# Attention on one core: the transposes of a tile's weights issued in front of the scores of the tile three ahead

## The reference, cut to what matters

```python
def one_chunk(args):
    j, q_j = args                       # 64 queries, the 8 chunks before them and their own
    k_j = lax.dynamic_slice_in_dim(k_pad, j * CHUNK, BAND, axis=1)
    v_j = lax.dynamic_slice_in_dim(v_pad, j * CHUNK, BAND, axis=1)
    s = jnp.einsum('bqhd,bkhd->bhqk', q_j, k_j) * scale + bias
    s = jnp.where(valid, s, jnp.float32(-1e30))
    p = jax.nn.softmax(s, axis=-1)
    return jnp.einsum('bhqk,bkhd->bqhd', p, v_j)
...
o = o * jax.nn.silu(g)                  # gate; then a product with w_out
```

## Time and profile before

| what | value |
|---|---|
| median of 3 runs | 2435.27 us (2433.29 to 2435.69) |
| profiled execution, first to last instruction (span) | 2432.2 us |
| PE, PEld busy | 2397.0 us (99%), 2050.3 us (84%) |
| DVE, ACT, POOL busy | 1591.1 us (65%), 1173.4 us (48%), 1212.6 us (50%) |
| chain that ended last, share on PE | 85% |
| mean granted TensorE clock | 0.997 |

### The profile page before, as it was taken

One profiled execution on the slowest core, in us unless ns is written; L12 is line 12 of the kernel. 1 busy time (PEld: TensorE's weight loads), 2 busy tenths in 40 slices (PEclk: granted clock), 3 DMA queues, 4 the chain that ended last, 5 costly groups with the idle time before them and its releaser, 6 DMA issues.

```text
span 2432.2 us, 36012 instructions
## 1 busy us (share of the span) xinstructions
PE 2397.0 (99%) x13552; PEld 2050.3 (84%) x13552; DVE 1591.1 (65%) x2151; ACT 1173.4 (48%) x2308; POOL 1212.6 (50%) x883
## 2 busy tenths in 40 slices
PE   7999999999999999999999999999999999999999
PEld 6888898875578898899888889999988888888887
DVE  6966757488544286653667775777434489888863
ACT  5322223334444253322445556788534434888861
POOL 1644445431044445544455545666444546866664
PEclk9999999999999999999999999999999999999999
DMA  7454544494133344543333448665234253300034
GB/s 278 156 192 150 188 152 160 152 314 143 36 108 127 129 153 153 190 158 113 104 104 104 104 117 234 160 155 144 76 115 165 99 173 111 104 1 1 5 127 156
DMA packets 295724, 329.21 MB, mean 135 GB/s; under 512 B 88264, under 2 KB 226304, under 8 KB 293760
## 3 DMA queue, kind: packets, MB, share of 16 engines
q1 hardware_dynamic: 294080, 326.81, 41.9%
q10 hardware_dynamic: 1472, 0.10, 0.0%
HBM read 247.53 MB, written 79.33 MB: 134 GB/s over the span
## 4 chain that ended last, share of the span: by engine, by line
PE 85%; DVE 7%; ACT 3%; issue 2%; DMA 1%; POOL 1%; SPq 0%; DVEq 0%; ACTq 0%
PE ps L1239 22%; PE ps L1241 22%; PE ps L1240 22%; PE ps L1576 3%; PE ps L1747 2%; PE ps L1728 2%; PE ps L1491 2%; PE ps L1510 2%; PE ps L1562 2%; PE ps L1504 1%; DVE s_raw L2433 1%; PE ps L1259 1%; PE ps L1474 1%; PE ps L1447 1%; DVE s_lo L2420 1%
## 5 line engine op out<-in xcount | busy, mean ns | idle before, releaser
L1125 POOL TENSOR_TENSOR w_lo<-raw,w_hi 128x512 fp32r<-128x512 f32 (+1 forms) x450 | 643.4, 1438 | 798.9 <-ACT w_hi L1853 762.9
L1853 ACT ACTIVATE w_hi<-raw 128x512 fp32r<-128x512 f32 (+1 forms) x454 | 281.3, 628 | 776.2 <-PE ps L1241 628.8
L1239 PE MATMUL ps<-w_hi,s_hi 128*128 128x256 f32 (+2 forms) x832 | 262.8, 316 | 0.6 <-DVE u L2553 0.3
L1240 PE MATMUL ps<-w_lo,s_hi 128*128 128x256 f32 (+2 forms) x832 | 262.0, 315 | 0.0
L1241 PE MATMUL ps<-w_hi,s_lo 128*128 128x256 f32 (+2 forms) x832 | 262.0, 315 | 0.0
L1125 POOL TENSOR_TENSOR w_lo<-raw_wide,w_hi 128x512 fp32r<-128x512 f32 x112 | 157.1, 1412 | 149.6 <-ACT w_hi L1853 149.6
L2553 DVE TENSOR_TENSOR u<-u,ps 128x1024 f32<-128x1024 f32 (+1 forms) x96 | 116.4, 1212 | 142.4 <-PE ps L1241 138.8
L1239 PE MATMUL ps<-w_hi,a_hi 128*128 128x256 f32 (+2 forms) x624 | 197.0, 316 | 0.6 <-POOL w_lo L1125 0.6
L1240 PE MATMUL ps<-w_lo,a_hi 128*128 128x256 f32 (+2 forms) x624 | 196.6, 315 | 0.0
L1241 PE MATMUL ps<-w_hi,a_lo 128*128 128x256 f32 (+2 forms) x624 | 196.6, 315 | 0.0
L1239 PE MATMUL ps<-s_hi,w_hi 128*128 128x512 f32 x480 | 188.6, 393 | 3.2 <-DVE s_lo L2420 2.3
(11 more groups left out here) (349 smaller groups left out, 6244.2 us busy)
## 6 DMA issues: line engine op xcount, KB each, us to landing
raw<-in_w SPq DMA_DIRECT2D x158, 512.0 KB, 4.2
ada_c<-in_ada SPq DMA_DIRECT2D x14, 2304.0 KB, 10.5
blk<-u SPq DMA_DIRECT2D x46, 512.0 KB, 4.3
raw_wide<-in_w SPq DMA_DIRECT2D x32, 512.0 KB, 4.6
blk<-c SPq DMA_DIRECT2D x23, 512.0 KB, 3.3
blk<-m1s SPq DMA_DIRECT2D x23, 512.0 KB, 3.3
ada_first<-in_ada SPq DMA_DIRECT2D x12, 768.0 KB, 16.2
r_g<-blk SPq DMA_DIRECT2D x8, 1024.0 KB, 9.3
```

The costliest lines, as they stand in the source:

```text
L1125: pool.tensor_tensor(w_ring(w_lo, n), w_source(n), w_ring(w_hi, n).bitcast(F32), ALU.subtract)\
L1239: pe.matmul(out, a_hi_, b_hi_, start=first, stop=False, skip_group_check=True)
L1240: pe.matmul(out, a_hi_, b_lo_, start=False, stop=False, skip_group_check=True)
L1853: act.activation(w_ring(w_hi, n), w_source(n), ACT.Copy).then_inc(w_rounded, 1)
```

## The change

In every step e of the loop the call of `a_scores(e + 3)` moves from the first to the second place, behind `a_turn(e)` and the one wait of step 0. Nothing is added or removed; no other queue is edited.

```diff
                 a_scores(2)
                 for e in range(AH * NT):
-                    if e + 3 < AH * NT:
-                        a_scores(e + 3)
                     if e == 0:
                         pe.wait_ge(ev, evicted(27, "c12"))
                     a_turn(e)
+                    if e + 3 < AH * NT:
+                        a_scores(e + 3)
                     if e:
                         a_values(e - 1)
                 a_values(AH * NT - 1)
```

## The result

The changed kernel takes **2439.65 us** (median of ten runs, 2438.34 to 2441.48) against 2434.06 us (2432.49 to 2435.69) of the kernel before on the same chip: 5.6 us more, ratio 1.0025, 95% interval 1.0015 to 1.0034. The forecast was 2440.3 us. It counted from 2435.27 us, the median of three runs of the kernel before; the median of ten lies 1.2 us lower.

What follows compares the result with a forecast made beforehand. TensorE, busy 99% of the span, was taken as the bound. Terms 2.9 - 0.4 + 0.8 + 0.7 + 0.7, with small waits 5.0 us, on the span 2432.2 plus 3.1 around it gave 2440.3 us; range 2437 to 2447.

Steps and rivals of the forecast that it cites:

- The bound: In plain attention heads TensorE alone sets the time, busy for all 15.39 us, so the move can only cost there.
- T3 in plain heads: Slot 3's transposes wait 0.36 us for GpSimd's late weights, 0.42 with the late weight load; 2.9 us in seven heads.
- the terms 0.70, 0.11 and 0.45: At T3: 0.70 us earlier without S6 in front, weights up to 0.11 later behind T0, less 0.45 of slack.
- They hold: Transposes in the other slots keep enough slack: narrow ones lose 0.9 to 1.2 of 1.6 us and more.
- Long heads: Heads 5, 7, 9, 11, 13: VectorE sets their length and absorbs slot 3's cost; -0.08 us each, -0.4 in all.
- ScalarE's copy at T0: T0 waits for the copy of T7 after late loads: 0.5 us at head 6, 0.1 to 0.2 in three more, 0.7 together.
- Head 0: S6 no longer runs during T3's wait for a load but behind it, at a slow clock: 0.8 us more.
- Heads 1 and 2: GpSimd is busy without a break, so earlier losses are swallowed and S6 is left over: 0.7 us more.
- The closed loop: Rival, chance 0.15: scores hang on transposes in a two-step round, every head loses 0.6 to 1.2 us more; 2453 us.
- Not slower: Rival, chance 0.14: earlier transposes and copies bring weights earlier, deciding from 0.36 us at slot 3; 2435.6 us.
- The longer slow stretch: Rival, chance 0.09: head 0's clock stays at half rate 2 to 4 us more, costing 1 to 2 us; 2442 us.

Runs made afterwards that it cites:

- run 2: Kernel before, with transposes ahead of scores in slot 3 of heads 1 to 15 alone; 2436.51 against 2433.0 us.
- run 3: Changed kernel, with the old order (scores first) in slot 0 of heads 1 to 15; 2437.49 against 2433.94 us.
- run 4: Changed kernel, with GpSimd's bias negation over 8 of 640 columns, so part of the computation is left out; 2434.94 against 2433.0 us.
- run 6: Changed kernel, with the old order (scores first) in slots 3 and 4 of heads 1 to 15; 2436.45 against 2433.94 us.
- run 7: Kernel before, with transposes ahead of scores in slot 6 of heads 1 to 15 alone; 2433.86 against 2433.94 us.
- run 11: Changed kernel, with VectorE's output split in heads 5, 7, 9, 11, 13 moved from slot 3 to slot 7; 2438.72 against 2433.65 us.
- run 8: Kernel before, with transposes ahead of scores in the eight steps of head 0 alone; 2433.39 against 2433.0 us.
- run 5: Kernel before, old order, with GpSimd's bias negation over 8 of 640 columns, so part of the computation is left out; 2431.09 against 2433.65 us.
- run 1: Changed kernel, with the old order (scores first) in slot 3 of heads 1 to 15 alone; 2437.19 against 2433.0 us.
- run 10: Kernel before, old order, with VectorE's output split in heads 5, 7, 9, 11, 13 moved from slot 3 to slot 7; 2431.54 against 2433.65 us.
- run 9: Kernel before, with transposes ahead of scores in step 3 of head 0 alone; 2435.06 against 2433.94 us.

## Why the prediction was right, and where its steps were not

**The total and its base.** The forecast of 2440.3 us missed by 0.65, and that is closer than its parts. It counted from 2435.27 us, where ten runs gave 2434.06, and added 5.0 where 5.6 were measured: one error of +1.2 and one of -0.6. In every run for which both are on record the time lies 1.8 to 1.9 us above the span of the same execution, so of the 3.1 us added to the span only that much was start and end; the rest was the difference between two executions.

**The bound.** Right: plain heads had no idle TensorE time, and all that the change brought was waits.

**T3 in plain heads.** Right in mechanism and in the wait, 0.36 expected and 0.36 measured, from the terms 0.70, 0.11 and 0.45; runs 2 and 3 confirm the middle one at 0.10 to 0.12. Mis-sized was the term of a plain head: 0.42 expected, 0.50 measured, 3.5 instead of 2.9 us in seven. Behind the negation a second wait lay ready, as run 4 shows: VectorE's inverse gives slot 3's weights only 0.36 us earlier.

**The step that failed: "They hold".** The other slots were judged by the slack that they had in the old order. Slot 6 came to the edge. In head 2 and in all plain heads T6 starts 0.06 us behind its weights, the least there is, so its weight load is late and it costs 0.05: its row of four takes 0.65 instead of 0.60. These rows of head 8 show why, first the changed kernel, then the one before.

```profile
1625.80 0.68 DVE L2939 TENSOR_TENSOR a_klo<-a_k,a_khi 128x512 fp32r<-128x512 f32 x1
1625.96 2.79 POOL L1191 TENSOR_TENSOR a_p<-a_p,st 128x512 f32<-128x512 f32 x2 [0.55 <-DVE st L2981]
...
1627.44 0.65 PE L1562 MATMUL ps<-ident,a_p 128*128 128x128 f32 x4
```

```profile
1623.19 1.04 POOL L1191 TENSOR_TENSOR a_p<-a_p,st 128x512 f32<-128x512 f32 x1 [0.21 <-DVE st L2981]
...
1623.57 1.21 DVE L2939 TENSOR_TENSOR a_klo<-a_k,a_khi 128x512 fp32r<-128x512 f32 x1 [0.46 <-ACT a_khi L2187]
```

The second row covers two instructions, the weights of slot 6 (1625.96 to 1627.38) and, from 1627.50, slot 7's. The duration of slot 6's weights was taken as fixed, and it wasn't: with VectorE's split started 0.16 us ahead of it, it took 1.42 instead of 1.04 us. In run 6, where GpSimd starts first again, they took 1.04, ended 0.76 ahead of T6, and T6's row was 0.60. So 0.42 in slot 3 and 0.05 in slot 6 make 0.47 of the 0.50; of the other 0.03 run 6 leaves 0.02 to the new junctions.

**Long heads.** Expected -0.08 each, measured +0.02, +0.03 and +0.08 in heads 7, 9 and 13; in heads 5 and 11 a late load hides the rest. S1's wait is gone, as said, and the wait of slot 3 was absorbed (runs 7 and 11), but T5 still waits 0.19 where none was expected. T4 costs 0.07 that wasn't expected either: its weights, which take 1.81 us beside VectorE's output split, now end 0.06 ahead of it. The saving of S1 goes into these two. The term of -0.4 should have been about 0.

**ScalarE's copy at T0.** Expected 0.5 at T0 of head 6 and 0.1 to 0.2 in three more. T0 of head 6 has none: the load came in time in this execution, and head 5 is 0.15 shorter than before. T0 waits 0.38, 0.12 and 0.47 in front of heads 11, 12 and 13. The heads that hold these waits (10, 11, 12) grow by 0.43, 0.20 and 0.24 beyond what the others of their kind do; less the 0.15 of head 5 that is 0.7, as forecast, but in other places. T0 of head 11 in the changed kernel:

```profile
1663.77 0.26 ACT L2216 ACTIVATE a_pT<-ps 128x128 f32<-128x128 f32 x1
...
1664.17 0.30 PE L1562 MATMUL ps<-ident,a_p 128*128 128x128 f32 x1 [0.21 <-ACT a_pT L2216]
```

Mechanism right; which heads it strikes is a matter of when loads land, and the eleven runs had it in different ones.

**Head 0.** Expected +0.8, measured -0.53 in the changed kernel. Read at one clock the term is right. From the start of the fifth transpose of T3 to the last V instruction of the head, the executions with head 0 in the new order and no slow stretch in it take 12.51 to 12.52 us (changed kernel, runs 6, 8 and 11); those with the old order and no slow stretch take 11.67 and 11.70 (runs 2 and 5). That is +0.84. With a slow stretch it is 13.1 to 13.7 (runs 1, 3 and 4) against 12.3 to 12.5 (kernel before, runs 7 and 10). Run 9 moves the one step and shows +0.58.

Two things that the forecast took as given hid this term. The slow stretch was missing in the changed kernel, so that part took 12.52 against 12.31, only 0.21 more. And the part ahead of it, from the start of the stage to that transpose, was 0.74 shorter: its end hangs on a load that came at nearly the same time in both (ScalarE's split starts at 1489.75 and 1489.64), while the stage started 0.85 later. Over the thirteen profiled executions that part takes 10.7 to 12.5 us. What decides whether the clock falls stays open: run 2 keeps the old order in head 0, has a pause of 1.81 us, and had the clock at 1.00 where the kernel before had 0.54.

```profile
1491.40:1495.00 3.60, 3.40 (x28) 3.11 (x27) 2.71 (x11) 3.41 (x10) 2.45 (x2) 1.00 0.83 222
```

The timing of run 8, +0.4 us with an interval of -2 to +2.7, can't tell a cost of 0.8 from none.

**Heads 1 and 2.** Expected 0.7, measured 0.34: T3 of head 2 waits 0.72 and its cost is +0.43, while head 1 is 0.09 shorter.

**The sum.** Heads 3 to 15: expected 2.9 - 0.4 + 0.7 = 3.2, measured 4.35. Heads 0 to 2: expected 1.5, measured -0.2. The late start of 0.85 belongs to heads 0 to 2, since head 0 took it up in its wait for the load: head 2 ends 0.66 us later than before, where 1.5 was expected. So one part came 1.2 too small and the other 0.8 too large, and they nearly cancel. That the forecast of 5.0 lies so near the span's 4.95 is luck beside a right mechanism.

**The rivals.** The closed loop is refuted: it asked for waits in front of T1, T5 or T7 in plain heads, and the changed kernel has none there; run 4 shows how near it was, with slot 3's weights waiting for VectorE and T3 0.01 late. "Not slower" asked for the weights of slot 3 to come 0.36 earlier; in head 8 GpSimd still finished them 1.35 us behind the negation and 0.30 behind the point at which T3 could start. The longer slow stretch appeared in no execution: behind the longest pause, 2.53 us in run 9, it is as long as before. The Trainium skill ("TensorE: Matmul & The Clock Gate", Part 1, What's actually happening) calls the throttled state the default and says that activity releases it; no run here shows that by that rule a longer pause makes a longer stretch. In the changed kernel the stretch is missing.

**What stays open.** The timed difference is 5.6 us, the profiled one 4.95, in an execution whose attention stage started 0.85 later; runs 10 and 11 differ by 7.2 timed and 4.6 profiled. The traces explain some 4 us of the stage by waits that have a place; for the rest there is the spread between executions and no more. Why the clock fell in head 0 in seven of the thirteen profiled executions and not in the other six is open too.

## What to carry to other kernels

On an engine that works in order and is the bound, moving a piece that waits ahead of a piece that doesn't takes away the wait's cover: for every piece so advanced, compare its slack with the length of what it passes, and add by how much its input comes later because other pieces moved too (0.70 + 0.11 - 0.45 here). Don't mix the two orders from one step to the next without going through the bank copies between them: the pattern that undid the costly step alone had a new wait of 0.17 us. Where another engine sets the length, a change to the order looks free and the gain lies elsewhere: moving VectorE's split by four slots brought 2.1 us (0.2 to 4.4), more than any choice of order did.

## What the runs showed of the hardware

GpSimd's product and VectorE's split of the keys, each with two inputs, don't run beside one another at full speed. When GpSimd's product had started first (1623.19), VectorE's split took 1.21 us and GpSimd's 1.04; when VectorE's had (1625.80), it took 0.68 and GpSimd's 1.42. The sums of waiting and working fit one of them standing still: VectorE's split ended 0.55 us behind the end of GpSimd's product, and in the other order GpSimd's ended 0.90 behind VectorE's. The Trainium skill ("SBUF — State Buffer", SBUF: two separate sides) says that the two engines share a pair of ports under an exclusive lock, and whichever starts first keeps it for the whole instruction; the trace agrees, with 0.13 us less than the full length left for the one that waited.

TensorE's clock after a pause is not a function of that pause's length alone. Behind the wait at the fifth transpose of T3 in head 0 the granted clock fell to 0.50 where that pause was 1.70, 1.83, 1.91, 1.94, 2.02, 2.18 and 2.53 us (runs 1 and 10, the kernel before, runs 3, 7, 4 and 9), and it stayed at 1.00 where it was 0.37, 1.07, 1.48, 1.72, 1.81 and 1.94 us (run 8, the changed kernel, runs 6, 11, 2 and 5). Two pauses of 1.94 us ended differently.

A transpose row of four or five that starts 0.05 to 0.06 us behind its weights costs 0.05 to 0.06 us more than one whose weight load ran ahead (0.77 instead of 0.71 for five, 0.65 instead of 0.60 for four): the step from its first transpose to its second is 0.16 instead of 0.11. It costs this with a wait in front of it (T3 in the changed kernel) and with none (T6 there, T3 in run 4).
